# A second feed-forward's down projection by seven block products per unit, with its inner width in three chunks

## What is computed

```python
D_MODEL, SEQ, D_FF_2 = 1024, 512, 2816

def conv_ffn(h, w_up, conv_w, conv_b, w_down):
    u = causal_dwconv(h @ w_up, conv_w, conv_b)      # 3 taps
    g, val = u[..., :D_FF_2], u[..., D_FF_2:]
    return (jax.nn.gelu(g, approximate=True) * val) @ w_down

# second_block, the end
h = rms_norm(x, pre_ffn_g[l]) * (1.0 + sc2) + sh2
y = conv_ffn(h, w_up[l], ffn_conv_w[l], ffn_conv_b[l], w_down[l])
x = x + g2 * rms_norm(y, post_ffn_g[l])
```

## Time and profile before

| what | value |
|---|---|
| three runs, median | 1698.19 us |
| lowest and highest of them | 1694.87 and 1702.92 us |
| span of the profiled execution | 1702.3 us |
| TensorE, busy | 1641.6 us, 96% |
| VectorE, ScalarE, GpSimd, busy | 51%, 40%, 48% |
| mean granted TensorE clock | 0.984 of 2.4 GHz |
| second feed-forward, first FU matmul to the end | 1327 to 1702.3 us |

### The profile page before, as it was taken

How to read it: one execution, slowest core, us unless ns; L and a number is a source line. 1 busy time by engine, 2 the same in 40 slices (tenths; PEclk the granted TensorE clock), 3 DMA queues, 4 the chain that set the end, 5 groups by cost and what they waited for, 6 DMA issues and landing times.

```text
span 1702.3 us, 21913 instructions
## 1 busy us (share of the span) xinstructions
PE 1641.6 (96%) x8026; PEld 1368.0 (80%) x8026; DVE 873.8 (51%) x1222; ACT 681.1 (40%) x1103; POOL 816.0 (48%) x670
## 2 busy tenths in 40 slices
PE   5998999999999999999999999989999999999997
PEld 5776888888878888888888889768878888888886
DVE  7556554556575345644335534666356655013324
ACT  3554444445233322542124323255645544334431
POOL 1373655646455544444554554332255454444443
PEclk7998999999999999999999999989999999999999
DMA  8221222122235545244545542211103142232221
GB/s 320 74 75 50 75 75 83 66 77 98 75 114 191 178 148 204 94 158 166 184 172 198 198 149 75 78 64 61 50 26 124 68 145 97 101 121 89 86 99 65
DMA packets 36825, 194.40 MB, mean 114 GB/s; under 512 B 4080, under 2 KB 6384, under 8 KB 21488
## 3 DMA queue, kind: packets, MB, share of 16 engines
q1 hardware_dynamic: 25200, 151.06, 24.5%
q10 hardware_dynamic: 11520, 41.95, 7.3%
HBM read 190.90 MB, written 2.10 MB: 113 GB/s over the span
## 4 chain that ended last, share of the span: by engine, by line
PE 81%; DVE 10%; ACT 4%; issue 2%; POOL 1%; DMA 1%; DVEq 0%; ACTq 0%; SPq 0%; POOLq 0%
PE main L903 60%; PE main L899 7%; PE main L896 2%; PE auxD L1214 2%; DVE tmp L2013 1%; DVE ada_first L2181 1%; ACT w_hi L1438 1%; PE main L1003 1%; DMA x<-x_in 1%; DVE tmp L2578 1%; PE auxD L1279 1%; DVE ysum L2283 1%; POOL w_lo L723 1%; PE auxC L1207 1%; PE auxB L1201 1%
## 5 line engine op out<-in xcount | busy, mean ns | idle before, releaser
L723 POOL TENSOR_TENSOR w_lo<-raw,w_hi 128x512 fp32r<-128x512 f32 x521 | 693.3, 1362 | 714.3 <-ACT w_hi L1438 710.5
L903 PE MATMUL main<-h_hi,w_hi 128*128 128x512 f32 (+1 forms) x1016 | 401.6, 395 | 1.0 <-DVEq L2080 1.0
L903 PE MATMUL main<-h_hi,w_lo 128*128 128x512 f32 (+1 forms) x1016 | 397.9, 392 | 0.0
L903 PE MATMUL main<-h_lo,w_hi 128*128 128x512 f32 (+1 forms) x1016 | 397.9, 392 | 0.0
L1438 ACT ACTIVATE w_hi<-raw 128x1024 fp32r<-128x1024 f32 (+2 forms) x267 | 257.9, 1014 | 249.6 <-PE main L903 175.4
L903 PEld LDWEIGHTS main<-h_hi,w_hi 128*128 128x128 f32 (+1 forms) x1016 | 191.8, 189 | 41.9 <-issue 2.3
L903 PEld LDWEIGHTS main<-h_hi,w_lo 128*128 128x128 f32 (+1 forms) x1016 | 191.6, 189 | 41.6
L903 PEld LDWEIGHTS main<-h_lo,w_hi 128*128 128x128 f32 (+1 forms) x1016 | 191.9, 189 | 39.8
L2156 DVE SCALAR_TENSOR_TENSOR tmp<-main,par,tmp 128x511 f32<-128x511 f32 x88 | 65.9, 749 | 161.8 <-ACT tmp L1550 160.0
L2181 DVE SCALAR_TENSOR_TENSOR ada_acc<-ada_raw,cs,ada_acc 128x1024 f32<-128x1024 f32 x70 | 104.9, 1499 | 35.3 <-DMA ada_raw<-w_ada 25.9
L2013 DVE SCALAR_TENSOR_TENSOR tmp<-main,half,tmp 128x511 f32<-128x511 f32 (+2 forms) x96 | 71.8, 748 | 43.1 <-ACT tmp L1459 40.8
(11 more groups left out here) (526 smaller groups left out, 2860.3 us busy)
## 6 DMA issues: line engine op xcount, KB each, us to landing
raw<-stream SPq DMA_DIRECT2D x118, 1024.0 KB, 4.8
ada_raw<-w_ada ACTq DMA_DIRECT2D x80, 512.0 KB, 4.4
ada_first<-w_ada SPq DMA_DIRECT2D x16, 512.0 KB, 10.2
raw<-stream SPq DMA_DIRECT2D x8, 768.0 KB, 4.3
raw<-stream SPq DMA_DIRECT2D x8, 640.0 KB, 3.9
x<-x_in SPq DMA_DIRECT2D x4, 512.0 KB, 7.7
x<-x_in SPq DMA_DIRECT2D x1, 2048.0 KB, 9.4
out<-x SPq DMA_DIRECT2D x16, 128.0 KB, 1.8
```

What stands on the lines that cost most here:

```text
L723: nc.gpsimd.tensor_tensor(lo[:, a:b], raw[:, s, a:b], hi[:, a:b], ALU.subtract).then_inc(lo_done, 1)
L903: ins = nc.tensor.matmul(bank[0:n, :], w[:, k, col:col + n], a[:, ka_, :], start=start, stop=stop)
```

## The change

The down projection of a group is seen as a product of two matrices in 2 by 2 blocks. The weight block A has 256 output columns in two tiles of 128 and an even number of hidden tiles, taken in pairs: A11 and A12 are the first output tile with the even and with the odd hidden tiles, A21 and A22 the second. The hidden block B is split into even and odd hidden tiles and into two halves of 256 tokens. The four blocks of the result take eight products of such blocks. The changed kernel makes them with seven, after the known scheme: sums and differences of blocks are formed first (S1 = A21 + A22, S2 = S1 - A11, S3 = A11 - A21, S4 = A12 - S2, and T1 to T4 of the hidden blocks in the same manner), and sums of the products give the result.

- Units. The inner width goes in three chunks of 8, 8 and 6 tiles (`G2_CHUNKS`) in place of two halves of 11: 8 FU, 4 FD, 8 FU, 4 FD, 6 FU, 4 FD. 11 of the 12 FD units are `fast`: 7 products, each of kn/2 pairs, times 3 matmuls, all of 256 columns. The last one (the third chunk, output tiles 6 and 7) is made as before, in halves, with 6 hidden tiles.
- TensorE (`seven_products`): the products use three banks, x, z and y. The order is A11 by B11 (x), S1 by T1 (z), S2 by T2 (y), A12 by B21 (x), S3 by T3 (y), S4 by B22 (z), A22 by T4 (y). The fourth waits until ScalarE has copied the first out of its bank (`p1_out`), the fifth until VectorE has taken `u2`, the sixth for `q5`, the seventh for `c22`.
- Weights of a fast unit: ScalarE makes 7 high parts, each of kn/2 times 128 columns (`high_of_form`), in place of 2 instructions. GpSimd makes S3 and 4 low parts (`low_forms`), VectorE makes S1, S2, S4 in banks `auxA` and `auxC` and 3 low parts (`sum_form`, `low_of_sum`). S1, S2 and A11 lie in new buffers `wx_hi`, `wx_lo` over `ada_raw` and `ada_acc`. For that the last 8 pieces of the modulation product are made in 4 FU units, two in each, in place of 8.
- Hidden tiles: for each pair VectorE makes T1 to T4 (banks `auxB`, `auxD`), and both engines make high and low parts of seven forms (`hidden_forms`).
- Results: in a fast unit VectorE makes 6 instructions of 256 columns (`fast_unit`), ScalarE one, and in chunks 2 and 3 GpSimd adds three blocks to `ysum` (`add_blocks`). The squares for the last norm come in the three last FD units.
- Some semaphores are merged (`dt_made` and the like), with no step moved by it.

```diff
-G2_HALF = G2_TILES // 2
+G2_CHUNKS = ((0, 8), (8, 8), (16, 6))
...
+    for c, (m0, n) in enumerate(G2_CHUNKS):
+        u += [Unit("FU", "w_up_2", 0, KD, [(P * (m0 + i), P, 0), (D_FF_2 + P * (m0 + i), P, 0)], "h", tag=(c, i))
+              for i in range(n)]
+        u += [Unit("FD", "w_down_2", m0, n, [(256 * i, 256, 0)], "hidden2", tag=(c, i),
+                   halves=(c == 2 and i == 3), fast=not (c == 2 and i == 3)) for i in range(4)]
...
+                product("A11", B11, x_bank, every, start=True, done=mid_full)
+                product("S1", T1, z_bank, every, start=True, done=mid_full)
+                for ps in ((most, rest) if u.tag[1] == 0 else (every,)):
+                    product("S2", T2, y_bank, ps, start=True, done=mid_full)
+                    product("A12", B21, x_bank, ps, done=x_done, after=(p1_out, n + 1))
+                product("S3", T3, y_bank, every, done=mid_full, after=part_made(n, "u2"))
+                product("S4", B22, z_bank, every, done=z_done, after=part_made(n, "q5"))
+                product("A22", T4, y_bank, every, done=y_done, after=part_made(n, "c22"))
...
+            def all_sums(v):
+                sum_form(v, "S1")
+                sum_form(v, "S2")
+                low_of_sum(v, "S1")
+                sum_form(v, "S4")
+                low_of_sum(v, "S2")
+                low_of_sum(v, "S4")
...
+                if u.n + 1 < len(units) and units[u.n + 1].fast:
+                    for name in FORMS_HI:
+                        high_of_form(units[u.n + 1], name)
+                elif 1 < u.n < len(units) - 1 and u.n - 1 not in crossing:
                     split_hi(units[u.n + 1])
```

More of the change, by code:

```diff
@@ L194, in ada_slots @@
     slots += [n for n in range(dn1, dn1 + 2) for s in both] + [n for n in range(dn1 + 2, dn1 + 6)]
-    slots += [n for n in range(fu0 + 1, fu0 + 9)]
+    slots += [n for n in range(fu0 + 1, fu0 + 5) for s in both]
     assert len(slots) == 80
@@ L288, in plan_steps @@
     for pair in range(3):
-        (mid[at["FD"][10 + 2 * pair]] if pair < 2 else end[at["FD"][13]]).append(("sumsq", (6, pair)))
+        mid[at["FD"][9 + pair]].append(("sumsq", (6, pair)))
+    for n, u in enumerate(u for u in units if u.fast):
+        mid[u.n - 1].append(("forms", n))
+    for u in units:
+        if u.name == "FU" and u.tag[1] % 2:
+            end[u.n].append(("pair", (G2_CHUNKS[u.tag[0]][0] + u.tag[1]) // 2))
     last = []
@@ L397, in build @@
             part = alloc(s_ml, "part", [MH, MD + 1])
+        with ExitStack() as s_wx:
+            wx_hi, wx_lo = (alloc(s_wx, f"wx_{s}", [3, 512], F32R) for s in ("hi", "lo"))
         seg_first = alloc(ctx, "seg_first", [TC - 1, HG, P], F32R)
@@ L512, in cc, with dt_made @@
             return con[:, at + a:at + (n if b is None else b)]
+        DT_STEPS = ("rows", "turned", "gates", "sums", "segments", "last")
+        def dt_made(name):
+            return dt_step, DT_STEPS.index(name) + 1
         ident, tri, ones = cc("ident"), cc("tri"), cc("ones")
@@ L2784, in _ @@
                 run(before[u.n])
+                if u.fast:
+                    fast_unit(u, units[u.n + 1])
+                    continue
+                if u.n + 1 < len(units) and units[u.n + 1].fast:
+                    all_sums(units[u.n + 1])
                 if u.n in crossing:
```

418 lines of the change are left out of this document (335 added, 83 removed).

## The result

The changed kernel takes 1739.45 us (median of 5 runs, 1736.05 to 1746.2), the kernel before 1699.48 on the same chip (5 runs). The ratio is 1.0231, with a 95% interval of 1.0201 to 1.0262: **40 us slower**. The forecast was slower, 1720, in a range that ended at 1738. The direction came out, and the waits at the starts lie where they were foretold, but the foretold loss of 22 us is little more than half of the measured one. The profiled execution spans 1744.4 us against 1702.3.

A forecast was written before the change was run, and what follows sets the result against it. The prediction took TensorE, busy 96% of the span, to bound the kernel. Its terms, -8.6 + 24.5 + 1.5 + 4.1 + 0.3 = +21.8 us, gave 1720 us on the median of 1698.2, range 1703 to 1738.

The forecast's parts named there:

- matmuls: Down projection: 933 matmuls of 256 columns at 0.120 us replace 120.5 us of matmuls, a gain of 8.6 us.
- three first units, clock included: Starts of the three chunks: 24.5 us of TensorE waits, plus 1.5 us for a lowered clock behind them.
- other fast units: Fast units behind each chunk's first: small waits for `c22` and `u2`, 4.1 us together, with 0 and 12 as ends.
- first FU run: FU units with two modulation pieces each: VectorE at about 11 us in a unit of 10.9, costing nothing.
- last unit and tail: End of the kernel: column sums 0.8 us late, most of it given back, so 0.3 us.
- the wait for the first product's copy: Start of a chunk of 8 tiles: TensorE idles 6.1 us before the fourth product, due at 4.0.
- the walk through ScalarE's list: Start of a chunk: seven copies delay the last hidden tile to 5.9 us; the first product's copy ends at 9.9.
- even: Rival at chunk starts: waits cost only the shortest chain, +4.5 us in all, 1703 us; chance 0.13.
- faster case: Rival at chunk starts: signals come early enough, the 8.6 us gain stands, 1690 us; chance 0.05.
- the banks give a unit of slack, so nothing: FU units with doubled modulation pieces: a unit of slack in the banks absorbs VectorE's load, 0 us.
- The clock term: Behind the three chunk starts: idleness may halve the clock for 6 us, 0.5 us each, 1.5 in all.
- Overload: Rival in all fast units: GpSimd and VectorE block each other, about 1740 us, deciding from 1.6 us; chance 0.14.

The follow-up runs named there:

- e_thin: The changed kernel with VectorE's weight-block sums and their low parts made for 128 columns alone in all fast units but the first: 1732.69 us, ratio 1.0188.
- e_ada_thin: The changed kernel with seven of the last eight multiply-adds of the modulation done on 64 of their 1024 columns: ratio 1.0197.
- e_ada_before: The kernel before with the last eight multiply-adds of the modulation two per unit in four up units, not one in eight: ratio 1.0014.
- e_p1early: The changed kernel with ScalarE copying the first product of each chunk's first fast unit ahead of the last hidden tile's high parts: 1742.13 us, ratio 1.0241.
- e_warm: The changed kernel with 44 unread matmuls of 256 columns ahead of the fourth product in each chunk's first fast unit: 1740.2 us, ratio 1.0227.
- e_order: The changed kernel with VectorE's low part of S1 put behind u2 and that of S4 behind c22, in each fast unit: 1738.79 us, ratio 1.0216.

## Why the prediction was right and wrong

From the first matmul behind the norm on, the loss is 419.1 - 380.1 = 39.0 us. By the prediction's own terms:

| term | foretold | read | what showed it |
|---|---|---|---|
| matmuls | -8.6 | -8.6 | units of 10.08 in e_thin, 0.120 apart |
| three first units, clock included | 26.0 | 30.6 | 19.81 + 20.28 + 18.21 - 27.72 |
| other fast units | 4.1 | 8.2 | 10.81 four times, 10.08 twice, 10.90, 9.51 |
| first FU run | 0 | 8.1 | 100.5 against 92.4 in the kernel before |
| last unit and tail | 0.3 | 0.6 | 24.1 - 72 x 0.120 against 30.7 - 132 x 0.120 |

What was read sums to 38.9. The last row counts from the first matmul of the last group to the end, less its matmuls: in the last unit TensorE waits 1.12 us ahead of the column sums (L1115 at 1727.68), which the shorter tail behind it gives back in part.

- **Right: the direction, the matmul term, and the wait for the first product's copy.** The idle stretches of 5.84, 5.66 and 5.52 us lie where the walk through ScalarE's list put them. The even and the faster case fell with them, as the copy ends 10.0 us behind the start instead of at 7.7 or within 4.
- **Wrong: "the banks give a unit of slack, so nothing".** This step failed, and it is the largest miss: 8.1 us where nothing was put. It counted VectorE's work per unit, but not what stands behind it on ScalarE: the next unit's weight split. e_ada_thin gives 6.3 of the 8.1 back, and e_ada_before shows that the same crowding costs 2.1 without the hidden forms. Part of the loss is the first chunk's start, which waits 1.94 us as its forms come late. In e_ada_thin it waits 1.06.
- **Mis-sized: the first units behind the copy, 4.6 us.** The walk gave 0.1 to 0.2 us for each hand-over. VectorE waits 0.24 to 0.32 even between two of its own dependent steps, and there are over ten of them up to `u2`. The fifth product comes 14.43 and 14.17 us behind the start against the 13.3 foretold, in the chunk of 6 tiles 13.35 against 12.0, and the seventh 18.28 against 16.7. The two theories that would free the start from this chain, the copy and the clock, left these times as they were (e_p1early, e_warm).
- **Mis-sized: the other units, 4.1 us.** VectorE was given 1.3 us of hand-overs in a unit. With 0.24 us at most of its twelve steps it needs about twice that. e_order moved `c22` one step ahead (10.47), e_thin thinned the steps (10.08). In the chunk of 6 tiles 5.3 us were lost against 3.5.
- **The clock term, 1.5 us, was about right in size as far as it could be tried, with a length that was too short.** The granted clock was 0.50 for 6.8, 10.2 and 10.2 us at the three starts, where 6 were assumed. It fell while TensorE was still idle, 1.9 to 3.6 us before the fourth product. TensorE was busy for 17.0 us of these stretches, so some 80 matmuls were slow, on paper 80 x 0.093 = 7.4 us. Keeping the clock gave 0.7 to 1.2 us at the one start where it could be kept throughout. The waits for `u2` and `c22` hid the rest, the first of them as foretold. The Trainium skill ("TensorE: Matmul & The Clock Gate", Part 1: The HAM clock gate) says that idleness brings the low clock, and all three starts agree. What it costs depends on who is waited for: next to nothing at the starts, 1.5 us in the third unit of e_order.
- **Overload, the rival with 1740 us, had nearly the right time and the wrong mechanism.** GpSimd stayed at 1.26 to 1.53 us for 512 columns in the fast units of 8 tiles, under the 1.6 from which it decides, and VectorE at 0.70. That its time fits is luck.

What stays open: the 1.8 us of the first FU run that e_ada_thin still has were not tried further (its timeline shows them as 1.2 us ahead of the first FD unit and 0.5 ahead of one low part). And no run takes VectorE's chain away from the starts, which carry most of the loss: that it bounds them is read from the timelines, from the unmoved times of the fifth product, and from the 1.7, 2.3 and 0.6 us that thinner steps gave.
